# First projections of a two-block transformer kernel: from rstd-scaled, column-form products to raw rows scaled on eviction

## The chip, the cores and the metric

The kernel runs on one core of a Trainium2 chip. The time is the device time of one execution in microseconds, the median of several runs; lower is better.

## What is computed

Two transformer blocks on one sequence of 256 tokens of width 1024, in 32-bit floats. The part around the change is the start of the first block, cut here from the reference:

```python
def rmsnorm(x, g):
    xf = x.astype(jnp.float32)
    y = xf * lax.rsqrt(jnp.mean(xf * xf, axis=-1, keepdims=True) + EPS)
    return (y * g.astype(jnp.float32)).astype(x.dtype)

h = rmsnorm(x, pre_mix_g[l])
aq, ak, av, hq, hf_fwd, hf_bwd, hi, hg = split_columns(h @ w_in[l], IN_SPLITS)
...
f = lb_dir + (1.0 - lb_dir) * jax.nn.sigmoid(z.astype(jnp.float32))
qf = heads(jax.nn.silu(q.astype(jnp.float32)), HG_HEAD_K)
o = bidirectional_gated_scan(qf, log_forget(zf_fwd, lb[0]), log_forget(zf_bwd, lb[1]), heads(i_in, HG_HEAD_V))
```

Here z is hf_fwd or hf_bwd and q is hq; the scan runs over the tokens in both directions. Then come cross attention to a memory `mem` of 256 rows, a feed-forward block with a convolution, and a second block of the same width.

## The kernel before

The sequence is two row tiles (R = 2) of 128 tokens; the width is eight tiles (KT = 8) of 128. Every 32-bit product is made of three: operands are split into a high part (rounded, fp32r) and a low part (the rest), and high x high, low x high and high x low are accumulated in PSUM. Weights come by SyncE's DMA queue into a ring of two slots of 2 MB, and are split in **pieces** of 128 x 1024 elements (512 KB): ScalarE's `ahead` writes the high part (L1630), VectorE's `ahead` the low part (L2265). Pieces are numbered in the order hff, hfb, hq, aq, akv, hi, hg, xkv0, ...; each of these has four, akv two. A piece has one of three places, so its high part waits until the piece three before it is used.

TensorE takes the pieces in two forms. `cols_half` (column form, L578 and L742) keeps a 128 x 128 weight tile stationary and streams the turned activations, 256 columns; the result has features on the partitions. A piece is 24 such products. `gemm_rows` (row form, L578 and L635) keeps the turned activations stationary and streams 512 weight columns; tokens are on the partitions. A piece is 12 products. A `turn` (L753) is four 128 x 128 transposes into one PSUM bank. Banks 0 to 3 (G) are for projections in turn, 4 to 7 (M) for turns, scores and scan levels; `take` waits until a bank's last readers are done.

Start: SyncE loads x, then the weights of hff and hfb; ScalarE issues the load of the columns (identity, gains) and, later, of the tables. ScalarE squares x by rows (L1646), GpSimd makes rstd (L1500, L1501), VectorE scales (L2277), TensorE turns (L775), ScalarE evicts high parts (L1661) and VectorE low parts (L2287) of `hT1`, with the gain. A few matmuls on zeros run meanwhile (L765). GpSimd issues the loads of the positions (L1528) and row vectors (L1530). Behind its first low parts VectorE makes the rotary angles (L2323 to L2342), which wait for tables and positions, then further low parts (L2343).

Then hff and hfb in column form, the turns of mem, and hq in column form. ScalarE applies sigmoid and silu on eviction (L1694); VectorE's `forget` makes f from it (L2365), ScalarE the keys 1 - f (L1729), GpSimd products of f over blocks (L1541). The scan works in nine levels (L830, L816): each is 32 or 16 small matmuls, behind which VectorE doubles queries (L2421) and keys (L2411) and keeps the result (L2396, L2388), and ScalarE gathers keys (L1723). To hide this, TensorE gets projection pieces as filler behind each level (`after_level`). Behind level 8 come the turns of q and k of the attention, one filler, and the value products of the scan (L872, L874).

## Time and profile before

| | |
|---|---|
| median of 3 runs | 892.42 us (892.14 to 893.91) |
| span of the profiled execution | 891.2 us (its own time is not listed) |
| TensorE busy | 879.5 us, 99% |
| VectorE busy | 648.1 us, 73% |
| ScalarE busy | 494.0 us, 55% |
| GpSimd busy | 92.7 us, 10% |
| read from memory | 150.35 MB, 170 GB/s over the span |
| first product of hff | 11.89 us |
| level 0 of the scan | 53.09 us |
| first value product of the scan | 114.80 us |

In the rows below, the first two numbers of a timeline row are the start and the length in us; "x16" is the number of instructions merged; brackets give how long the engine was idle before and what ended it. PE is TensorE's matmuls, PEld its weight loads, DVE VectorE, ACT ScalarE, POOL GpSimd, SP SyncE; an engine's name with a q is its instruction queue, where DMAs are issued. Names such as sb_ta are tiles in SBUF (sb_ta holds `hT1`), ps are PSUM banks.

### The profile page before, as it was taken

The page shows a single profiled execution, that of the slowest core. Times are in us where ns is not written, and L with a number is a line of the kernel's source. Part 1 is how long each engine was busy: PE and PEld are TensorE (multiplying, and loading weights), DVE is VectorE, ACT ScalarE, POOL GpSimd, SP SyncE. Part 2 cuts the span into 40 slices and gives each one's busy share as a digit, 9 for nine tenths or more (in the row PEclk, how much of TensorE's full clock was granted, in tenths as well). Part 3 has the DMA queues.
Part 4 walks back from the last instruction along what each step waited for, and adds up shares of the span by engine and source line. Part 5 has one row for each costly group of instructions (what it writes and reads, how often), then busy time and mean ns, then how long its engine had stood idle before and what let it go on. Part 6 is the DMA issues. An engine that isn't in the chain of part 4 may idle for free.

```text
span 891.2 us, 13262 instructions
## 1 busy us (share of the span) xinstructions
PE 879.5 (99%) x5100; PEld 753.7 (85%) x5100; DVE 648.1 (73%) x1024; ACT 494.0 (55%) x880; POOL 92.7 (10%) x123
## 2 busy tenths in 40 slices
PE   8999999999999999999999999999999999999997
PEld 6988897889889888888789887898888888888885
DVE  5789975574879688789856846677787774766774
ACT  5954665464577465566635366676555772324341
POOL 1324100000010000000133300011030100000000
PEclk9999999999999999999999999999999999999999
DMA  9755424453664455556418644344366554564531
GB/s 317 245 168 176 155 95 139 146 201 106 189 212 143 142 181 186 201 188 238 166 60 286 210 142 142 107 166 166 96 232 193 175 180 142 189 212 166 189 142 48
DMA packets 99502, 152.25 MB, mean 171 GB/s; under 512 B 2608, under 2 KB 66352, under 8 KB 99184
## 3 DMA queue, kind: packets, MB, share of 16 engines
q1 hardware_dynamic: 99040, 150.68, 50.6%
q8 instruction: 41, 0.67, 0.3%
q10 hardware_dynamic: 288, 0.47, 0.2%
q0 software_dynamic: 112, 0.26, 0.1%
q14 instruction: 21, 0.17, 0.1%
HBM read 150.35 MB, written 1.05 MB: 170 GB/s over the span
## 4 chain that ended last, share of the span: by engine, by line
PE 90%; DVE 5%; ACT 2%; issue 1%; DMA 1%; POOL 0%; DVEq 0%; POOLq 0%; SPq 0%; ACTq 0%
PE ps L578 27%; PE ps L571 19%; PE ps L1079 13%; PE ps L635 7%; PE ps L1083 7%; PE ps L667 4%; PE ps L742 2%; PE ps L753 1%; DVE sb_wlo L2265 1%; PE ps L830 1%; ACT sb_whi L1630 1%; PE ps L706 1%; PE ps L1027 1%; PE ps L931 1%; PE ps L1223 1%
## 5 line engine op out<-in xcount | busy, mean ns | idle before, releaser
L2265 DVE TENSOR_TENSOR sb_wlo<-sb_ring,sb_whi 128x1024 fp32r<-128x1024 f32 (+2 forms) x169 | 203.6, 1216 | 81.2 <-ACT sb_whi L1630 80.8
L1630 ACT ACTIVATE sb_whi<-sb_ring 128x1024 fp32r<-128x1024 f32 (+2 forms) x169 | 174.0, 1045 | 101.3 <-PE ps L635 70.0
L578 PE MATMUL ps<-sb_whi,sb_tb 128*128 128x512 f32 (+2 forms) x520 | 137.7, 387 | 0.0
L578 PEld LDWEIGHTS ps<-sb_whi,sb_tb 128*128 128x128 f32 x520 | 94.1, 188 | 17.2 <-issue 1.0
L635 PE MATMUL ps<-sb_wlo,sb_tb 128*128 128x512 f32 (+2 forms) x224 | 66.6, 380 | 0.0
L578 PE MATMUL ps<-sb_whi,sb_ta 128*128 128x512 f32 (+1 forms) x240 | 61.4, 380 | 0.0
L1518 POOL TENSOR_SCALAR sb_st<-sb_st 128x1 f32<-128x1 f32 x14 | 7.3, 524 | 451.6 <-ACT sb_probs L1894 451.5
L2223 ACT ACTIVATE sb_b<-sb_b 128x512 f32<-128x512 f32 x9 | 5.7, 632 | 79.7 <-DVE sb_b L2694 79.7
L578 PEld LDWEIGHTS ps<-sb_whi,sb_ta 128*128 128x128 f32 x240 | 42.4, 188 | 8.6 <-issue 0.5
L635 PEld LDWEIGHTS ps<-sb_wlo,sb_tb 128*128 128x128 f32 x224 | 41.5, 188 | 7.8
L2694 DVE TENSOR_REDUCE sb_b<-ps 128x256 f32<-128x512 f32 x36 | 23.9, 686 | 28.6 <-PE ps L1083 28.6
L1997 ACT ACTIVATE sb_b<-ps 128x256 f32<-128x256 f32 x32 | 12.2, 381 | 52.7 <-PE ps L1083 52.7
L571 PE MATMUL ps<-sb_whi,sb_ta 128*128 128x512 f32 (+1 forms) x120 | 37.4, 377 | 0.1
L578 PE MATMUL ps<-sb_tb,sb_whi 128*128 128x256 f32 x256 | 35.1, 288 | 0.8 <-DVE sb_tb L2287 0.7
L578 PEld LDWEIGHTS ps<-sb_tb,sb_whi 128*128 128x128 f32 x256 | 32.0, 191 | 2.5 <-issue 1.6
L1709 ACT ACTIVATE sb_b<-ps 128x512 f32<-128x512 f32 (+1 forms) x44 | 24.2, 590 | 9.6 <-PE ps L742 4.6
L578 PE MATMUL ps<-sb_ta,sb_whi 128*128 128x256 f32 x192 | 26.6, 294 | 1.4 <-DVE sb_ta L2287 1.4
L2265 DVE TENSOR_TENSOR lent9lo<-sb_ring,lent9hi 128x1024 fp32r<-128x1024 f32 x19 | 23.2, 1220 | 5.9 <-ACT lent9hi L1630 5.9
L2265 DVE TENSOR_TENSOR lent1lo<-sb_ring,lent1hi 128x1024 fp32r<-128x1024 f32 x18 | 22.0, 1221 | 7.5 <-ACT lent1hi L1630 7.5
L635 PE MATMUL ps<-sb_wlo,sb_ta 128*128 128x512 f32 (+1 forms) x96 | 27.3, 372 | 0.0
L2754 DVE SCALAR_TENSOR_TENSOR sb_b<-sb_b,sb_col 128x255 f32<-128x255 f32 x64 | 26.6, 478 | 0.8 <-ACT sb_b L2015 0.8
L578 PEld LDWEIGHTS ps<-sb_ta,sb_whi 128*128 128x128 f32 x192 | 25.1, 201 | 1.7 <-issue 1.6
(430 smaller groups left out, 2065.0 us busy)
## 6 DMA issues: line engine op xcount, KB each, us to landing
sb_ring<-in_w_in SPq DMA_DIRECT2D x32, 1024.0 KB, 5.6
sb_ring<-in_w_up SPq DMA_DIRECT2D x18, 1024.0 KB, 5.1
sb_ring<-in_w_down SPq DMA_DIRECT2D x11, 1024.0 KB, 7.2
sb_ring<-in_w_ffn_down SPq DMA_DIRECT2D x11, 1024.0 KB, 7.5
sb_ring<-in_w_ffn_gate SPq DMA_DIRECT2D x9, 1024.0 KB, 5.3
sb_ring<-in_w_ffn_up SPq DMA_DIRECT2D x9, 1024.0 KB, 5.4
sb_ring<-in_w_xkv SPq DMA_DIRECT2D x8, 1024.0 KB, 5.6
sb_ring<-in_w_out SPq DMA_DIRECT2D x4, 1024.0 KB, 5.0
```

The costliest lines, as they stand in the source:

```text
L571: mm = pe.matmul(o, l[a_], r[b_], start=(start and n == 0), stop=(stop and n == 2), skip_group_check=not check)
L578: pe.matmul(o, l, r, start=(start and n == 0), stop=False, skip_group_check=True)
L635: mm = pe.matmul(o, T[0][:, k0 + i, r * P:(r + 1) * P], w[1][:, i], start=False, stop=k0 + i == k - 1, skip_group_check=True)
L667: mm = pe.matmul(o, T[0][:, k0 + i, r * P:(r + 1) * P], w[1][:, i], start=False, stop=k0 + i == k - 1, skip_group_check=True)
L742: mm = pe.matmul(o, w[1][:, i, :], T[0][:, i, :], start=False, stop=i == KT - 1, skip_group_check=True)
L1079: pe.matmul(o[:, :], w[0][:, k, :], both_halves[f][:, k].rearrange("p two n -> p (two n)"), start=k == 0, stop=False)
L1083: mm = pe.matmul(o[:, 0:S], w[1][:, k, :], T[0][:, k, :], start=False, stop=k == KT - 1)
L1630: act.activation(piece_pair(m)[0], src, ACT.Copy).then_inc(s("hi_done"), 1)
L1709: act.activation(dst, bank[banks.at[key][0]][:, 0:n], ACT.Copy, scale=1.0 if scale is None else scale).then_inc(banks.release(key), 1)
L2265: dve.tensor_tensor(low, pieces[m][1], high.bitcast(F32), ALU.subtract).then_inc(s("lo_done"), 1)
L2694: dve.tensor_reduce(dst[c], o[:, :].rearrange("p (two n) -> p n two", two=2), AX.X, ALU.add).then_inc(banks.release(key), 1)
L2754: dve.scalar_tensor_tensor(dst, src, COL[:, at:at + 1], dst, ALU.mult, ALU.add).then_inc(banks.release(key) if last and c and i < SPLIT_FR ...
```

## The change

The host passes a turned copy of x with the gains in front. ScalarE and VectorE split it, times the gain, straight into `hT1`, without rstd; the first chunk's loads are spread over ScalarE's and SyncE's queues. All projections of x are in row form on these unscaled tiles; rstd is the `scale` of the activation that evicts. The sigmoid of hff and hfb and the silu of hq are evicted as rows and turned by TensorE; `forget` reads the turned gates in PSUM, and turned hq is evicted by ScalarE. Plain x is still loaded, for its squares and the residual. The pieces behind the levels move one forward, and the columns, tables, positions and row vectors are loaded at other places.

```diff
+        turned_x = nc.alloc_sbuf_tensor_at("turned_x", [P, KT + KT * S], F32, offset=nc.sbuf_base - 4 * KT * 2 * S)
+        first_gain, xT = turned_x[:, 0:KT], turned_x[:, KT:].rearrange("p (k n) -> p k n", n=S)
+        hff_rows, hfb_rows, hq_rows = v3(B[1], 0, R, 512), v3(B[1], R * 512, R, 512), v3(B[2], NS, R, 512)
...
-        T_FORM = ("hff", "hfb", "hq", "xkv0", "xkv1", "w_xq0", "w_xq1")
+        FIRST = "hff"
+        T_FORM = ("xkv0", "xkv1", "w_xq0", "w_xq1")
+        def first_chunk(name, w):
+            slot_at[0] += 1
+            raw[name] = [v3(ring, q * PIECE, 2, 512) for q in range(4)]
+            chunks.append((name, [((q // 2,), [(raw[name][q], w[2 * q * P:2 * (q + 1) * P, :])]) for q in range(4)], KT, 512))
...
-            for cols in (512, 512, 512, 256):
+            for cols in (512, 512, 256):
...
-            for m in range(4):
-                banks.take(pe, f"pre_mix_g.{m}", M[m], 2)
-            for r in range(R):
-                for m in range(4):
-                    if m % 2 == 0:
...

+                piece_at[0] = 1
+                keys = [f"{FIRST}.{r}" for r in range(R)]
+                for key in keys:
+                    banks.take(pe, key, next_g())
+                def both_rows(k, T, w):
+                    for r, key in enumerate(keys):
+                        mm = pe.matmul(bank[banks.at[key][0]][:, :], T[:, k, r * P:(r + 1) * P], w[:, k, :],
+                                       start=k == 0 and T is hT1[0] and w is high, stop=False, skip_group_check=True)
+                    return mm
+                for k in range(2):
+                    pe.wait_ge(*(hi_done(0) if k else (s("first_w_hi"), 1)))
+                    pe.wait_ge(s("first_hi"), k + 1)
+                    both_rows(k, hT1[0], high)
+                    pe.wait_ge(s("first_lo"), k + 1)
+                    both_rows(k, hT1[1], high)
+                    pe.wait_ge(*(lo_done(0) if k else (s("first_w_lo"), 1)))
+                    mm = both_rows(k, hT1[0], low)
+                piece_used(0, mm)
+                for k in range(2, KT):
+                    waits_at[k, None] = [(s("first_lo"), k + 1)]
+            def turn_gate(name, src, at):
+                for r in range(R):
+                    pe.wait_ge(*banks.empty(f"{name}.{r}"))
+                for m in range(2):
+                    turn(f"{name}T.{m}", src, [2 * m, 2 * m + 1], M[at + m], 1)
+            first_piece()
+            gemm_rows("hff", hT1, (1, 4))
+            gemm_rows("hfb", hT1)
+            pe.wait_ge(s("col_in"), 16)
+            turn_gate("hff", hff_rows, 0)
+            gemm_rows("hq", hT1, (0, 2))
+            turn_gate("hfb", hfb_rows, 2)
+            gemm_rows("hq", hT1, (2, 4))
             turn_norm("mem_norm_g")
-            for half in range(2):
-                cols_half("hq", hT1, half)
+            gemm_rows("aq", hT1, (0, 1))
+            turn_gate("hq", hq_rows, 0)
+            gemm_rows("aq", hT1, (1, 2))
...
-            gemm_rows("aq", hT1, (0, 1))
-            after_level(0, (gemm_rows, "aq", hT1, (1, 3)))
-            after_level(1, (gemm_rows, "aq", hT1, (3, 4)), (gemm_rows, "akv", hT1, (0, 1)))
-            after_level(2, (gemm_rows, "akv", hT1, (1, 2)), (gemm_rows, "hi", hT1, (0, 1)))
-            after_level(3, (gemm_rows, "hi", hT1, (1, 3)))
-            after_level(4, (gemm_rows, "hi", hT1, (3, 4)), (gemm_rows, "hg", hT1, (0, 1)))
-            after_level(5, (gemm_rows, "hg", hT1, (1, 3)))
-            after_level(6, (gemm_rows, "hg", hT1, (3, 4)), (turned_tiles, "mem_norm_g"),
-                        (cols_half, "xkv0", memT, 0, (0,)))
-            after_level(7, (cols_half, "xkv0", memT, 0, (1,)), (cols_half, "xkv0", memT, 1, (0,)))
-            after_level(8, (turn_qk1,), (cols_half, "xkv0", memT, 1, (1,)))
+            after_level(0, (gemm_rows, "aq", hT1, (2, 4)))
+            after_level(1, (gemm_rows, "akv", hT1))
+            after_level(2, (gemm_rows, "hi", hT1, (0, 2)))
+            after_level(3, (gemm_rows, "hi", hT1, (2, 4)))
+            after_level(4, (gemm_rows, "hg", hT1, (0, 2)))
+            after_level(5, (gemm_rows, "hg", hT1, (2, 4)))
+            after_level(6, (turned_tiles, "mem_norm_g"), (cols_half, "xkv0", memT, 0))
+            after_level(7, (cols_half, "xkv0", memT, 1))
+            after_level(8, (turn_qk1,))
...
+            for q in range(4):
+                part = slice(KT * (q > 0) + 2 * q * S, KT + 2 * (q + 1) * S)
+                sp.dma_start(turned_x[:, part], a["turned_x"][:, part]).then_inc(s(f"turned_x_in{q}"), 16)
+            load_part(FIRST, 2)
+            load_part(FIRST, 3)
+            load_part("hfb", 0)
             for r in range(R):
                 sp.dma_start(x[:, r, :], a["x"][r * P:(r + 1) * P, :]).then_inc(s(f"x_in{r}"), 16)
-            load_all(names[:SLOTS])
+            load_part("hfb", 1)
+            load("hq")
             sp.dma_start(mem, a["mem"].rearrange("(r p) n -> p r n", p=P)).then_inc(s("mem_in"), 16)
             sp.dma_start(masks[:, :, :], a["masks"].rearrange("p (l n) -> p l n", n=BLOCK)).then_inc(s("masks_in"), 16)
-            load_all(names[SLOTS:])
+            load_all(names[SLOTS + 1:])
             o = out.rearrange("(r p) n -> p r n", p=P)
...
+            pool.wait_ge(s("first_hi"), KT)
             pool.dma_start(posi[:, :], a["positions_2"].rearrange("(r p) -> p r", p=P),
                           allow_slow_non_contiguous=True).then_inc(s("pos_in"), 16)
             pool.dma_start(SG[:, :], a["row_vectors"].partition_broadcast(P)).then_inc(s("sg_in"), 16)
+            for r in range(R):
+                sums, rstds = (t[:, r:r + 1] for t in stats["pre_mix_g"])
+                rstd("pre_mix_g", [(s("pre_mix_g_sq"), r + 1)], sums, D, rstds)
...
-            act.dma_start(ident_col[:, :], a["ident_col"]).then_inc(s("col_in"), 16)
+            for k in range(2):
+                act.dma_start(raw[FIRST][0][:, k, :], chunks[0][1][0][1][0][1][k * P:(k + 1) * P, :]
+                              ).then_inc(s(f"first_half_in{k}"), 16)
+            dst, w = chunks[0][1][1][1][0]
+            act.dma_start(dst, w.rearrange("(k p) n -> p k n", p=P)).then_inc(raw_sem[FIRST, 1], 16)
...
+                high = piece_pair(0)[0]
+                hi_at[0] = 1
+                for k in range(KT):
+                    if k < 2:
+                        act.wait_ge(s(f"first_half_in{k}"), 16)
+                        act.activation(high[:, k, :], raw[FIRST][0][:, k, :], ACT.Copy
+                                       ).then_inc(s("hi_done" if k else "first_w_hi"), 1)
+                    if k % 2 == 0:
+                        act.wait_ge(s(f"turned_x_in{k // 2}"), 16)
+                    act.activation(hT1[0][:, k, :], xT[:, k, :], ACT.Copy, scale=first_gain[:, k:k + 1]
+                                   ).then_inc(s("first_hi"), 1)
+                    if k in (3, 5, 7):
+                        ahead_of(FIRST, (k + 1) // 2)
+                    if k == 5:
+                        act.dma_start(ident_col[:, :], a["ident_col"]).then_inc(s("col_in"), 16)
+                        act.dma_start(cst[:, :], a["tables"]).then_inc(s("const_in"), 16)
+            first_tiles()
+            ahead_of("hff", 6)
+            for r in range(R):
+                act.wait_ge(s(f"x_in{r}"), 16)
...
             act.wait_ge(s("angles"), 2)
             act.activation(ropes[:, :, 0:32], ang[:, 0], ACT.Sin).then_inc(s("sincos"), 1)
             act.activation(ropec[:, :, 0:32], ang[:, 1], ACT.Sin).then_inc(s("sincos"), 1)
-            ahead_of("hff", 5)
+            ahead_of("hff", 7)
             act.wait_ge(s("lam_dots"), 1)
             act.activation(lam_e, lam_dot, ACT.Exp).then_inc(s("lam_exp"), 1)
             act.wait_ge(s("lb_shift"), 2)
             act.activation(lb_e, lb_e, ACT.Exp).then_inc(s("lb_exp"), 1)
+            ahead_of("hff", 8)
+            for r in range(R):
+                act.wait_ge(s("pre_mix_g_rstd"), r + 1)
+            def apply(name, r, dst, func):
+                key = f"{name}.{r}"
                 act.wait_ge(*banks.full(key))
-                act.activation(dst, bank[banks.at[key][0]][:, 0:512], func).then_inc(banks.release(key), 1)
+                act.activation(dst[:, r, :], bank[banks.at[key][0]][:, 0:512], func, scale=rstd1(r)
+                               ).then_inc(banks.release(key), 1)
+            for r in range(R):
+                apply("hff", r, hff_rows, ACT.Sigmoid)
+            ahead_of("hfb", 6)
+            for r in range(R):
+                apply("hfb", r, hfb_rows, ACT.Sigmoid)
+            ahead_of("hfb", 7)
+            def spread_keys(d, n):
                 for half in range(2):
-                    ahead_of("hfb", 5 + 2 * half)
-                    apply(f"hfb.{half}", FD[:, NS + half * 512:NS + (half + 1) * 512], ACT.Sigmoid)
-            pre_norm("mem_norm_g", mem, [[(s("mem_in"), 16)]] * R, memT, gain_at("mem_norm_g"), forget_hfb)
+                    act.wait_ge(*banks.empty(f"h{n}T.{half}"))
+                for half in range(2):
+                    lo = d * NS + half * 512
+                    act.activation(KD[:, lo:lo + 512], FD[:, lo:lo + 512], ACT.Identity,
+                                   bias=1.0, scale=-1.0).then_inc(s("k_ready"), 1)
+            spread_keys(0, "ff")
+            def before_mem():
+                ahead_of("hq", 4)
+                spread_keys(1, "fb")
+                ahead_of("hq", 5)
+                gather_keys(1)
+                for r in range(R):
+                    apply("hq", r, hq_rows, ACT.Silu)
...
+            pre_norm("mem_norm_g", mem, [[(s("mem_in"), 16)]] * R, memT, gain_at("mem_norm_g"), before_mem)
             ahead_of("hq", 6)
-            apply("hq.1", hq[:, 512:1024], ACT.Silu)
+            for m in range(2):
+                take_rows(f"hqT.{m}", hq[:, m * 512:(m + 1) * 512])
...
-                take_rows(f"aq.{r}", qkv[:, r, 0:512])
+                take_rows(f"aq.{r}", qkv[:, r, 0:512], scale=rstd1(r))
...
+            high, low = piece_pair(0)
+            lo_at[0] = 1
+            for k in range(KT):
+                if k < 2:
+                    dve.wait_ge(*(hi_done(0) if k else (s("first_w_hi"), 1)))
+                    dve.tensor_tensor(low[:, k, :], pieces[0][1][:, k, :], high[:, k, :].bitcast(F32),
+                                      ALU.subtract).then_inc(s("lo_done" if k else "first_w_lo"), 1)
+                dve.wait_ge(s("first_hi"), k + 1)
+                dve.scalar_tensor_tensor(hT1[1][:, k, :], xT[:, k, :], first_gain[:, k:k + 1],
+                                         hT1[0][:, k, :].bitcast(F32), ALU.mult, ALU.subtract).then_inc(s("first_lo"), 1)
+                if k in (3, 5, 7):
+                    ahead_of(FIRST, (k + 1) // 2)
             dve.wait_ge(s("col_in"), 16)
-            pre_norm("pre_mix_g", x, hT1, gain_at("pre_mix_g"), lambda: None, lambda: ahead_of("hff", 1))
-            ahead_of("hff", 4)
             dve.wait_ge(s("const_in"), 16)
             dve.tensor_copy(mask_rows[:, :], cst[:, C_QROW:C_QROW + 2 * P]).then_inc(s("mask_ready"), 1)
...
-            ahead_of("hfb", 1)
+            ahead_of("hfb", 2)
...
-                    dve.wait_ge(*banks.empty(f"h{name}.{half}"))
+                    key = f"h{name}T.{half}"
+                    o = psum(key)
-                        f = dve.tensor_scalar(t[:, j * S:(j + 1) * S], t[:, j * S:(j + 1) * S],
+                        f = dve.tensor_scalar(t[:, j * S:(j + 1) * S], o[:, j * S:(j + 1) * S],
                                               lb_left[:, c:c + 1], lb[:, c:c + 1], ALU.mult, ALU.add)
-                    f.then_inc(s(f"{name}_ready"), 1)
-            ahead_of("hfb", 3)
+                    f.then_inc(banks.release(key), 1)
+            ahead_of("hfb", 5)
             forget("ff", 0)
-            ahead_of("hfb", 5)
+            ahead_of("hfb", 7)
             def forget_hfb():
-                ahead_of("hq", 3)
                 forget("fb", 1)
+                ahead_of("hq", 5)
+                dve.wait_ge(s("k_ready"), 4)
+                dve.tensor_tensor(kdiag, KD[:, 0:NS], KD[:, NS:2 * NS], ALU.add).then_inc(s("kdiag"), 1)
             pre_norm("mem_norm_g", mem, memT, gain_at("mem_norm_g"), lambda: None, forget_hfb)
-            dve.wait_ge(s("k_ready"), 4)
-            dve.tensor_tensor(kdiag, KD[:, 0:NS], KD[:, NS:2 * NS], ALU.add).then_inc(s("kdiag"), 1)
-            ahead_of("hq", 5)
+            ahead_of("hq", 6)
```

## Rows read from the trace of the kernel before

**Rows 1.** The page: span, busy time of each engine, and the chain that ended last, by engine.
```profile
span 891.2 us, 13262 instructions
...
PE 879.5 (99%) x5100; PEld 753.7 (85%) x5100; DVE 648.1 (73%) x1024; ACT 494.0 (55%) x880; POOL 92.7 (10%) x123
...
PE 90%; DVE 5%; ACT 2%; issue 1%; DMA 1%; POOL 0%; DVEq 0%; POOLq 0%; SPq 0%; ACTq 0%
```

**Rows 2.** Stretches: start:end, length, busy of PE, PEld, DVE, ACT, POOL, clock, DMA share, GB/s.
```profile
2.70:10.00 7.30, 5.80 (x20) 2.89 (x20) 2.56 (x8) 3.54 (x6) 3.02 (x6) 1.00 1.08 339
6.70:11.90 5.20, 2.36 (x17) 1.74 (x17) 4.04 (x8) 3.98 (x9) 2.88 (x5) 1.00 1.14 327
12.30:15.60 3.30, 3.30 (x17) 3.18 (x16) 3.30 (x7) 2.44 (x4) 0.00 (x0) 0.50 1.09 341
16.40:53.00 36.60, 36.41 (x294) 35.53 (x292) 28.33 (x62) 28.89 (x44) 12.65 (x14) 1.00 0.64 210
50.00:70.00 20.00, 20.00 (x186) 17.09 (x185) 15.68 (x20) 10.00 (x13) 0.00 (x0) 1.00 0.70 237
70.00:100.00 30.00, 29.92 (x249) 24.61 (x249) 29.72 (x46) 15.80 (x23) 14.41 (x6) 1.00 0.45 141
```

**Rows 3.** TensorE's timeline: first piece, fifth piece, level 0, value products.
```profile
11.89 3.62 PE L578 MATMUL ps<-sb_ta,sb_whi 128*128 128x256 f32 x16 [1.35 <-DVE sb_ta L2287]
...
25.06 2.08 PE L578 MATMUL ps<-sb_ta,sb_whi 128*128 128x256 f32 x16
...
53.09 1.15 PE L830 MATMUL ps<-sb_b 128*64 128x64 f32 x32
...
114.80 0.27 PE L872 MATMUL ps<-sb_b 128*128 128x128 f32 x1
```

**Rows 4.** Groups of ScalarE's instructions from 0 to 60 us.
```profile
L1630 ACT ACTIVATE sb_whi<-sb_ring 128x1024 fp32r<-128x1024 f32 x17 | 17.8, 1068 | 8.4 <-PE ps L635 4.2 <-PE ps L742 3.5 <-DMA sb_ring<-in_w_in 0.6
L1694 ACT ACTIVATE sb_b<-ps 128x512 f32<-128x512 f32 x6 | 3.5, 594 | 1.2 <-PE ps L742 1.2
L1661 ACT ACTIVATE sb_ta<-ps,sb_col 128x256 fp32r<-128x256 f32 x8 | 3.0, 488 | 0.6 <-PE ps L775 0.6
...
L1694 ACT ACT_TABLE_LOAD x2 | 2.6, 1283 | 0.0
L1723 ACT ACTIVATE sb_b<-sb_b 128x512 f32<-128x512 f32 x4 | 2.5, 698 | 0.5 <-DVE sb_b L2411 0.5
```

**Rows 5.** TensorE's timeline: a column piece, turns of mem, halves of a row piece.
```profile
22.18 2.08 PE L578 MATMUL ps<-sb_ta,sb_whi 128*128 128x256 f32 x16
...
36.93 1.96 PE L753 MATMUL ps<-sb_col,sb_b 128*128 128x128 f32 x16 [0.19 <-DVE sb_b L2277]
38.65 2.16 PE L578 MATMUL ps<-sb_ta,sb_whi 128*128 128x256 f32 x16
...
57.02 1.07 PE L578 MATMUL ps<-sb_whi,sb_ta 128*128 128x512 f32 x4
...
58.38 1.07 PE L578 MATMUL ps<-sb_whi,sb_ta 128*128 128x512 f32 x4
```

**Rows 6.** Loads issued from 0 to 60 us: KB each, us from issue to landing.
```profile
sb_b<-in_mem SPq DMA_DIRECT2D x1, 1024.0 KB, 13.1
...
sb_cst<-in_tables ACTq DMA_DIRECT2D x1, 272.0 KB, 6.2
...
sb_posi<-in_positions POOLq DMA_DIRECT2D x1, 1.0 KB, 5.6
```

**Rows 7.** Timelines of GpSimd, VectorE and ScalarE: positions, angles, sine, a low part.
```profile
8.66 0.95 POOL L1528 DMA_DIRECT2D sb_posi<-in_positions  x1
...
18.92 0.29 DVE L2323 CAST sb_maskrows<-sb_cst 128x256 bf16<-128x256 f32 x1
...
22.03 0.26 ACT L1680 ACTIVATE sb_ropes<-sb_probs 128x64 f32<-128x64 f32 x1 [2.98 <-DVE sb_probs L2342]
...
52.32 1.22 DVE L2265 TENSOR_TENSOR sb_wlo<-sb_ring,sb_whi 128x1024 fp32r<-128x1024 f32 x1
```

100 lines of the change are left out of this document (37 added, 63 removed).

## Prediction

> **What bounds the kernel now.** I read the page first: TensorE is busy 99% of the span and its instructions are 90% of the chain that ended last [rows 1]. So time is won or lost where TensorE starts late, waits, or gets more or less work; other engines matter where they feed it. Next I read the granted clock and the data rate of the start [rows 2], then TensorE's timeline [rows 3]. The first product of the first projection starts at 11.89 us, its fifth weight piece at 25.06, level 0 of the scan at 53.09 and the scan's value products at 114.80. After that TensorE hardly waits, so a shift at 114.80 should reach the end. The clock stood at 1.2 GHz from 12.3 to 15.6, after a stretch in which TensorE was busy 2.36 of 5.20 us. Lastly, VectorE is busy 29.72 of 30 us between 70 and 100 [rows 2]: inside the scan it is nearly a second bound.
>
> The profiled execution, whose own time isn't listed, has a span of 891.2 us, 1.2 below the median of the runs, 892.42; I take that 1.2 as constant. From no change a measurement of this kernel can tell about 0.2%, 1.8 us.
>
> **Removed at the start.** The path x, squares, rstd, scaling, 16 transposes, eviction ended at 11.89. Now TensorE needs the first quarter of turned x and a 256 KB weight block. The start moves 339 GB/s from 2.7 us on [rows 2]. Together these are 0.53 MB, so they land at about 4.5; ScalarE's half piece (0.6, as an eviction of 512 columns) and tile (0.38) give first products at about 5.6 [rows 4]. Weight piece 1 is behind 2.1 MB in all, lands near 9.0, and its high part takes 1.07: 10.1. Pieces 2 and 3 land near 10.5 and 12.0, ahead of need.
>
> **Row form against column form.** A half piece in row form takes 1.36 us, from 57.02 to 58.38, so a piece takes 2.73; a column piece takes 2.88, from 22.18 to 25.06 [rows 5]. That is only 0.15 a piece, 1.65 for the eleven pieces of hff, hfb and hq behind the first. Against it stand 24 new transposes: 16 took 1.72 us (36.93 to 38.65) [rows 5], so 24 take 2.6, with six starts of groups 3.1. The form by itself loses 1.4; all gain must come from the start.
>
> **The new wait.** TensorE runs pieces 1 to 3 from 10.1 to 18.6 (3 x 2.73 and 0.3 for a low part) and the first four products of piece 4 (0.9) until 19.5. Then it wants piece 4's low part, which VectorE makes only after the rotary angles. These need the tables and the positions. Both loads are issued later than now. ScalarE issues the column and table loads behind turned tile 5 and piece 2: piece 1 until 10.1, tiles 10.8, piece 2 11.8, then two issues, taken at 0.4 each, GpSimd's being 0.95 [rows 7]: 12.6. The tables, issued at 12.2, take 6.2 us to land as now: 18.4 [rows 6]. GpSimd's positions load waits for all eight turned tiles (13.3) and takes 5.6 [rows 6]: 19.0. VectorE has finished piece 3 at 15.6 and stands still; behind it stand its angles, the low parts of 4 and 5, and ScalarE's sine. From the mask copy at 18.92 to the sine at 22.03 the angles took 3.1 us: 22.1, and with 1.22 for the low part [rows 7] TensorE goes on at 23.4. TensorE waits 3.9 us. In the kernel before, the positions were issued at 8.66 and landed some 5 us before VectorE came to them at 18.92: that cover is gone. Piece 4 thus behaves as if started at 22.5, against 25.06: of the 6.3 us of earlier start 2.6 are left.
>
> The least that the wait can be is 1.6, where both loads are there when VectorE is free (column vectors about 16, 0.65 for the bounds, 3.1 angles, 1.2 low part); at the most it is 3 us more than I take, should the loads queue as mem's did, which needed 13.1 us for 1 MB [rows 6]. I take the rows' own 5.6 and 6.2, as the queues are as full at 12 to 19 as they were at 6 to 15 (327 and 341 GB/s) [rows 2]. The Trainium skill, DMA: Bandwidth & Descriptors, section Anatomy of one DMA, gives a fixed cost of about 2.0 us and bytes over 436 GB/s; by it the positions land at 15.4 and my sum would be 2.3 us lower, no change. The rows of this start show nearly three times that for a load of 1 KB, and the measurement decides.
>
> **From piece 4 to level 0.** Before: 28.0 us (25.06 to 53.09) for eight column pieces, one row piece and the mem transposes. After: ten pieces (a second aq piece comes ahead of level 0) 27.3, gate turns 3.1, mem transposes 1.7, 0.2 for the start of the level, and waits. For the waits I laid ScalarE's queue out from hq's end H (about 46.8): it gathers keys (1.3), loads the Silu table (1.28) and evicts hq (2 x 0.55), since it is held before that by VectorE's forget of hfb; only then come eight mem tiles (8 x 0.38), the high part of aq's second piece (1.0) and the turned hq [rows 4]. That high part is ready near H + 6.9. TensorE has 1.7 + 2.73 + 1.0 = 5.5 of work until it wants it. So it waits about 1.4 there, split between the turns of hq (mem banks 0 and 1 must be emptied) and the piece; I add 0.3 for its low part and 0.5 for hq's last low part: 2.2, bounded by 0 (ScalarE an instruction earlier) and 4. Sum 34.5, level 0 at 57.0: 3.9 later than 53.09.
>
> **Moved and hidden.** The levels keep two pieces each, the last filler (2.88) behind level 8 goes away, because one piece more was done ahead of level 0: minus 2.9. Its cover isn't needed: turning q and k follows, and the level's eviction ends under it. In the levels VectorE comes to its query products about 1 us later against level 0 than now, as it sits behind the same turns, and has 20.0 minus 15.7 us of idle time in 50 to 70 [rows 2]: I take 1.3 of new waits, between 0 and 3. The x squares and rstd are hidden (x lands near 20, the rstd is there near 23, first use is at about 28 on ScalarE). ScalarE's queue gains three weight loads ahead of all else, the split of piece 0 (two halves of 0.6 for 1.07) and two evictions of turned hq (0.6 each); VectorE loses the four scalings of x, and its forget reads PSUM where it read SBUF, some 0.05 an instruction. Both had idle time in the stretch from 16.4 to 53 (28.89 and 28.33 of 36.6 busy) [rows 2], so only what lies on the way around H is charged. The second megabyte of x costs 3 us of transfer; that is paid in the landings above; later it is covered, as mem's load, issued within 10 us of the start, landed 13.1 later [rows 6] and was wanted near 36. Scaling on eviction replaces a constant. GpSimd's products of f start some 3 us later than now and aren't wanted until level 2. SP issues the four quarters of turned x ahead of everything, and plain x only behind half of hfb; nothing there is wanted sooner than it lands.
>
> **The clock.** In the row 2.36 busy us of 5.20 were followed by 3.3 us at 1.2 GHz, which cost half of them, 1.65 [rows 2]. The new standstill is 3.9 us: between 0 and 1.65, I take 0.4, as it is shorter. A fall at the start would be free: it is absorbed in the wait for piece 4. The Trainium skill, TensorE: Matmul & The Clock Gate, section PE-mode transpose, says that transposes don't count as busy; the stretch before the fall held only transposes, which agrees. By it the start stays at 2.4 GHz, which changes nothing in the sum.
>
> **Sum:** +3.9 + 1.3 - 2.9 + 0.4 = +2.7: 892.4 + 2.7 = 895.1 us.
>
> **Rivals.**
> Small loads early: tables and positions are there when VectorE wants them, 1.6 of wait in place of 3.9, and no fall of the clock. 892.4 - 2.3 - 0.4 + 2.7 = 892.4, no change. For it: the positions are 1 KB. Against: 5.6 us in the row. 0.2; with the forecast's spread this is nearly all of "same".
> TensorE is fed throughout (the other side): VectorE's angles don't hold piece 4 back, as lands and issues come some us earlier than I laid out, and the waits of 2.2 and 1.3 don't arise. Place: piece 4's low part; it decides from its end before about 20.5. 892.4 + 2.7 - 0.4 - 3.9 = 890.8, and with the other waits gone 887.3; I name 889.0. Chance 0.24. For it: VectorE works only 28.3 of 36.6 us from 16.4 to 53 [rows 2].
> The clock falls in full: the standstill is followed by 3.3 us at half rate, as before: 895.1 + 1.25 = 896.3, and with late small loads 898. Chance 0.2.
> The lead is swallowed in the scan: should level 0 come early, VectorE at 29.72 of 30 us holds the levels, and only the moved filler counts: 889.5. It lies within the second rival.
> That row form isn't in fact 0.15 cheaper, or turns cost 0.13 each as in small groups, moves the sum by under 1.
>
> **Numbers.** Forecast and its spread 0.36, small loads early 0.2, fed 0.24, clock 0.2. Faster by over 1.8 us: 0.24. Within 1.8: 0.23 (0.2, and a little of the forecast). Slower: 0.53. The range leaves out one in ten at each side: 888.8 to 897.6. Cases of both signs are near each other; the likeliest alone has 893.3 to 896.8.
>
> **What would show it.** First real product near 5.6, piece 1 near 10.1; a wait of TensorE for VectorE's low part of about 4 us ending near 23.4, and VectorE's idle time before the mask copy released by a DMA; row pieces of 2.73; six turns of 0.43 to 0.5; waits of 1 to 2 us around the turns of hq behind ScalarE; level 0 near 57.0; no piece between level 8 and the value products at 117. It is wrong if the tables and positions land before 16, if level 0 stands before 54, or if the levels take much more than 56 us.

## The result and the profile after

The changed kernel takes 897.10 us (median of 4 runs, 896.98 to 897.26) against 892.52 us of the kernel before on the same chip (4 runs, 892.14 to 893.91): ratio 1.0049, interval 1.0036 to 1.0061. It is slower, by 4.6 us; 2.7 were forecast. The spans of the two profiled executions differ by 4.1 us.

The page of the changed kernel, beside [rows 1]: span, busy time by engine, and the chain that ended last.

```profile
span 895.3 us, 13001 instructions
...
PE 880.7 (98%) x4962; PEld 745.3 (83%) x4962; DVE 647.2 (72%) x1021; ACT 496.4 (55%) x883; POOL 89.3 (10%) x123
...
PE 83%; DVE 8%; ACT 4%; DMA 2%; issue 2%; POOL 0%; ACTq 0%; DVEq 0%; POOLq 0%; SPq 0%
```

TensorE's share of the chain has fallen from 90% to 83%; VectorE's has grown from 5% to 8%, ScalarE's from 2% to 4% and DMA's from 1% to 2%, some 18 us. So I looked for waits that one of these three ends, and first for those that a DMA ends.

TensorE's timeline of the changed kernel, the lines that answer to [rows 3] and [rows 5] (pieces are numbered from 0, hff's four being 0 to 3):

```profile
6.33 1.36 PE L791 MATMUL ps<-sb_whi,sb_ta 128*128 128x512 f32 x4 [0.26 <-ACT sb_ta L1726]
...
10.38 1.18 PE L591 MATMUL ps<-sb_whi,sb_ta 128*128 128x512 f32 x4 [0.82 <-ACT sb_whi L1673]
...
13.58 1.07 PE L591 MATMUL ps<-sb_whi,sb_ta 128*128 128x512 f32 x4
...
18.27 1.20 PE L591 MATMUL ps<-sb_whi,sb_ta 128*128 128x512 f32 x4 [1.81 <-ACT sb_whi L1673]
...
23.01 1.16 PE L591 MATMUL ps<-sb_whi,sb_ta 128*128 128x512 f32 x4
...
46.78 0.74 PE L648 MATMUL ps<-sb_wlo,sb_ta 128*128 128x512 f32 x2 [1.21 <-DVE sb_wlo L2340]
...
55.42 1.19 PE L591 MATMUL ps<-sb_whi,sb_ta 128*128 128x512 f32 x4 [0.78 <-ACT sb_whi L1673]
...
58.74 1.15 PE L868 MATMUL ps<-sb_b 128*64 128x64 f32 x32
...
118.80 0.46 PE L908 MATMUL ps<-sb_b 128*128 128x128 f32 x2
```

The first real product starts at 6.33 in place of 11.89, and piece 2 at 13.58. Then the lead goes: piece 3 waits until 18.27 for ScalarE's high part, and piece 4 (hfb's first) starts only at 23.01. Level 0 starts at 58.74, 5.65 us later than before, and the value products at 118.80, 4.0 later. From there on nothing changes: 4.0 of the 4.1 us of the spans are there.

Piece 3 is late although its load is the sixth issue of SyncE's queue, behind the four quarters of turned x and part 2 of hff. SyncE's queue tells why; its timeline, and then the table of its waits:

```profile
2.57 11.85 SPq L1481 DMA_DIRECT2D sb_ring<-in_w_in  x3
14.47 0.98 SPq L1511 DMA_DIRECT2D sb_x<-in_x  x2
```

```profile
SPq L1481 <- DVE sb_wlo L2340: 13.2, 2, 10.3
```

Three issues cover 11.85 us, 10.3 of them a single wait for a low part that VectorE makes. It is `load_part("hff", 3)`. The bookkeeping of `raw_before` (L467 of the changed kernel) gives a load, as what it must wait for, the last load of the same half of the ring. Parts 2 and 3 of hff are both entered under half 1, though they fill different bytes of it, so part 3 waits until piece 2 has been split. Nothing needs that: it is a false wait. Behind it in the queue stand hfb's weights and x. The data rate has a hole for it:

```profile
GB/s 0 0 53 141 305 332 412 404 401 410 391 393 254 5 0 144 353 131 0 74 221 399 388 121 170 347 415 369 399 421 412 401 401 393 388 385 385 390 385 390
```

These are 40 slices of 0.75 us, so the rate is 5, 0 and 144 GB/s from 9.75 to 12, and again 0 and 74 from 13.5 to 15. Piece 3 lands at 17.2 and hfb's first half at 21.7.

The granted clock follows; stretches of the changed kernel, columns as in [rows 2]:

```profile
18.00:20.00 2.00, 1.66 (x5) 1.07 (x6) 1.71 (x6) 0.22 (x1) 0.00 (x0) 0.92 0.88 296
20.00:22.00 2.00, 2.00 (x6) 1.59 (x5) 1.76 (x11) 0.23 (x1) 0.00 (x0) 0.50 1.04 392
22.00:24.00 2.00, 2.00 (x7) 1.16 (x6) 1.86 (x7) 2.00 (x3) 0.00 (x0) 0.73 1.02 412
```

After the wait of 1.81 us piece 3 runs at 1.2 GHz for the most part and takes 4.74 us in place of 2.73. The last view is VectorE's timeline, beside [rows 7]:

```profile
18.25 1.23 DVE L2340 TENSOR_TENSOR sb_wlo<-sb_ring,sb_whi 128x1024 fp32r<-128x1024 f32 x1 [3.95 <-ACT sb_whi L1673]
...
19.75 0.28 DVE L2409 CAST sb_maskrows<-sb_cst 128x256 bf16<-128x256 f32 x1
...
22.86 2.36 DVE L2340 TENSOR_TENSOR sb_wlo<-sb_ring,sb_whi 128x1024 fp32r<-128x1024 f32 x2
```

VectorE stands still until 18.25, but it is ScalarE's high part of piece 3 that releases it and no small load. Then come the angles, and the low part of piece 4 is ready at 24.1. I had forecast 23.4, for another reason. So three things were candidates for the one stretch: the late landing, the angles with their loads ahead of the low part, and the clock. A second group of waits, at 46.78 and 55.42, stood around the turns of hq.

### The profile page after: what moved, and what is told of

Read it like the earlier page. It is cut to its first block, busy times and chain, and to the rows that moved or that the text cites. A ratio compares the mean times of both kernels' runs of the same rounds, so it can differ in the third digit from the quotient of the medians.

```text
span 895.3 us, 13001 instructions
## 1 busy us (share of the span) xinstructions
PE 880.7 (98%) x4962; PEld 745.3 (83%) x4962; DVE 647.2 (72%) x1021; ACT 496.4 (55%) x883; POOL 89.3 (10%) x123
## 4 chain that ended last, share of the span: by engine, by line
PE 83%; DVE 8%; ACT 4%; DMA 2%; issue 2%; POOL 0%; ACTq 0%; DVEq 0%; POOLq 0%; SPq 0%
PE ps L591 23%; PE ps L584 19%; PE ps L1115 13%; PE ps L1119 7%; PE ps L648 6%; PE ps L680 4%; DMA sb_ring<-in_w_in 2%; PE ps L755 2%; DVE sb_wlo L2340 2%; ACT sb_whi L1673 1%; PE ps L766 1%; PE ps L719 1%; PE ps L1063 1%; PE ps L967 1%; PE ps L1259 1%
## 5 line engine op out<-in xcount | busy, mean ns | idle before, releaser
L591 PE MATMUL ps<-sb_whi,sb_ta 128*128 128x512 f32 (+1 forms) x328 | 86.4, 388 | 3.4 <-ACT sb_whi L1673 3.4
L591 PEld LDWEIGHTS ps<-sb_whi,sb_ta 128*128 128x128 f32 x328 | 59.2, 190 | 16.9 <-ACT sb_whi L1673 4.9
L648 PE MATMUL ps<-sb_wlo,sb_ta 128*128 128x512 f32 (+1 forms) x140 | 42.5, 390 | 1.7 <-DVE sb_wlo L2340 1.5
L2072 ACT ACTIVATE sb_b<-ps 128x256 f32<-128x256 f32 x32 | 12.2, 381 | 52.7 <-PE ps L1119 52.7
L584 PE MATMUL ps<-sb_whi,sb_ta 128*128 128x512 f32 (+1 forms) x120 | 37.5, 377 | 0.1
L648 PEld LDWEIGHTS ps<-sb_wlo,sb_ta 128*128 128x128 f32 x140 | 25.3, 191 | 9.2 <-DVE sb_wlo L2340 4.6
L1792 ACT ACTIVATE sb_b<-ps 128x512 f32<-128x512 f32 x40 | 22.5, 606 | 7.5 <-PE ps L766 4.9
L584 PEld LDWEIGHTS ps<-sb_whi,sb_ta 128*128 128x128 f32 x120 | 21.9, 188 | 4.7 <-DVE sb_ta L2800 0.5
```

The source lines that it names most:

```text
L584: mm = pe.matmul(o, l[a_], r[b_], start=(start and n == 0), stop=(stop and n == 2), skip_group_check=not check)
L591: pe.matmul(o, l, r, start=(start and n == 0), stop=False, skip_group_check=True)
L648: mm = pe.matmul(o, T[0][:, k0 + i, r * P:(r + 1) * P], w[1][:, i], start=False, stop=k0 + i == k - 1, skip_group_check=True)
L1792: act.activation(dst, bank[banks.at[key][0]][:, 0:n], ACT.Copy, scale=1.0 if scale is None else scale).then_inc(banks.release(key), 1)
```

## The experiments

Level 0 and value products are read from TensorE's timeline of each run. The kernel before had medians of 892.46, 892.47, 892.70 and 892.81 us beside the four groups of runs.

### e1_no_false_wait, e2_small_loads_early, e3_both, e4_fix_low_first

e1 takes the false wait away:

```diff
                 if name == FIRST:
+                    raw_before[name, j] = []
```

e2 has only the small loads early: ScalarE issues columns and tables right behind its three weight loads, and GpSimd doesn't wait for the turned tiles.

```diff
-            pool.wait_ge(s("first_hi"), KT)
...
+            act.dma_start(ident_col[:, :], a["ident_col"]).then_inc(s("col_in"), 16)
+            act.dma_start(cst[:, :], a["tables"]).then_inc(s("const_in"), 16)
```

e3 has both. e4 has the edit of e1, and in place of earlier loads an altered order on VectorE:

```diff
+            ahead_of("hfb", 2)
             dve.wait_ge(s("const_in"), 16)
             dve.tensor_copy(mask_rows[:, :], cst[:, C_QROW:C_QROW + 2 * P]).then_inc(s("mask_ready"), 1)
```

> The changed kernel with one wait taken away: the fourth load of hff doesn't wait any more until VectorE has split the third (it goes to other bytes of the ring). In the changed kernel SyncE stood from about 3.5 to 13.54 us in that wait, and piece 3 of hff landed near 17. Theory A (two causes in series: behind the late load stand the late positions and tables): piece 3 lands near 12 to 13, TensorE no longer waits for it, but the positions still land near 19.8, VectorE's angles end near 22.9, and TensorE waits 4 to 4.5 us for the low part of piece 4 until about 24.1; piece 4 behaves as if started near 23.2 against 23.01 now, the clock falls behind that wait as it does now, and the time stays within 1 us of 897.1. Rival B (the late load is the only cause): the 1.8 us of standstill and the fall of the clock go, level 0 moves from 58.74 to about 55.2 and the time to about 893.6.

> The changed kernel with the small loads early: ScalarE issues columns and tables right behind its weight loads, GpSimd positions and row vectors at once. SyncE's false wait stays. Theory A: no gain by itself, since VectorE makes the angles behind the low part of piece 3, which still waits for its late load; the 0.7 MB more in the early queue may even push the weights back by up to 1 us. 896.6 to 898.1, level 0 between 58.3 and 59.8. Rival (the late positions are what held TensorE): piece 4 starts earlier and the time falls by 2 us or more, to 895 or below.

> Both together: no false wait and small loads early. Theory A: neither cause is left, so TensorE has no standstill over 1 us ahead of piece 5, the clock stays at 2.4 GHz, piece 4 starts near 19 instead of 23.01, and the 4 us come through to level 0 (about 54.7) and the end: 892.6 to 893.8. Rival C (ScalarE and VectorE, or the landings, are the next bound at once): piece 4 starts earlier but piece 5 to 8 wait for their parts, and less than half of it comes through: 895 or more.

> No false wait, small loads where the change put them, but VectorE makes the low parts of pieces 4 and 5 ahead of the angles. Theory A: TensorE doesn't hang on the positions any more; hfb's first half lands near 16.5, piece 4's low part is ready near 19, piece 4 starts near 19 to 19.5, the clock stays up, the time is as with both changes of the loads, 892.6 to 894. If the positions' place cost nothing (rival B), this is equal to the run that only takes the false wait away.

Measured: e1 896.49 us (5 runs), ratio to before 1.0040 (1.0027 to 1.0052). e2 897.69 (5 runs), 1.0054 (1.0042 to 1.0067). e3 894.48 (11 runs), 1.0020 (1.0011 to 1.0029). e4 892.19 (11 runs), 0.9992 (0.9983 to 1.0000).

The times of e1 and e2 lie in the range of their theory A. e3 is 0.7 us above its range and e4 0.4 us below.

In e1 the weights are there in time, and TensorE runs from 12.2 to 20.1 without a stop; then comes the wait that I had forecast. VectorE's and then TensorE's timeline of e1:

```profile
18.44 0.30 DVE L2410 CAST sb_maskrows<-sb_cst 128x256 bf16<-128x256 f32 x1 [1.49 <-DMA sb_cst<-in_tables]
```

```profile
22.88 0.73 PE L649 MATMUL ps<-sb_wlo,sb_ta 128*128 128x512 f32 x2 [2.81 <-DVE sb_wlo L2341]
```

The tables land at 18.4, to the tenth what the prediction said, but by luck: they were issued at 10.8 and not at 12.2, and took 7.6 us and not 6.2. Piece 4's low part is taken at 22.88. The 10.3 us of false wait were thus worth 0.6 us: what it held up was behind the angles anyway. The wait was also good for something. The loads of the changed kernel, and then of e1, KB each and us from issue to landing:

```profile
sb_cst<-in_tables ACTq DMA_DIRECT2D x1, 272.0 KB, 2.7
...
sb_col<-in_ident_col ACTq DMA_DIRECT2D x1, 187.0 KB, 2.5
```

```profile
sb_cst<-in_tables ACTq DMA_DIRECT2D x1, 272.0 KB, 7.6
...
sb_col<-in_ident_col ACTq DMA_DIRECT2D x1, 187.0 KB, 6.0
```

With SyncE's loads held back the small loads land in 2.5 and 2.7 us, with them running in 6.0 and 7.6. So each of the two faults hid the other: take one away and the other comes up. e2 shows it from the other side. Its small loads are early, the false wait keeps VectorE from piece 3 until 19.7, the angles come behind that, and it is even 0.6 us slower than the changed kernel, since columns and tables, issued right behind piece 1's weights, are now in flight beside them: these take 8.8 us to land in place of 7.6, and piece 1 starts at 11.56 in place of 10.38. e3 pays that 1.1 us too (piece 1 at 11.51), and comes to level 0 at 55.06 in its profiled execution, which took 893.52, 1.0 less than the median. e4 pays nothing. Its stretches, columns as in [rows 2]:

```profile
14.00:18.00 4.00, 4.00 (x19) 3.33 (x18) 3.03 (x7) 2.54 (x3) 0.96 (x2) 1.00 1.04 403
18.00:22.00 4.00, 4.00 (x20) 3.30 (x19) 3.65 (x16) 2.94 (x5) 1.68 (x4) 1.00 1.04 377
22.00:26.00 4.00, 4.00 (x19) 3.31 (x18) 2.50 (x8) 3.92 (x8) 0.00 (x0) 1.00 1.05 387
```

TensorE is busy throughout at 2.4 GHz, level 0 starts at 53.58 and the value products at 113.66. That is 5.1 us earlier than in the changed kernel, as the medians say (4.9). It is the prediction's second rival as far as piece 4 goes.

The same comparison prices the clock where the forecast wait stands alone. Stretches of e1 behind that wait, columns as in [rows 2]:

```profile
22.00:24.00 2.00, 1.12 (x4) 0.99 (x5) 2.00 (x3) 1.98 (x3) 0.00 (x0) 0.92 1.06 389
24.00:26.00 2.00, 2.00 (x6) 1.54 (x6) 1.93 (x6) 0.68 (x3) 0.00 (x0) 0.50 1.04 385
26.00:28.00 2.00, 2.00 (x8) 1.57 (x7) 1.08 (x3) 1.88 (x2) 0.00 (x0) 0.73 1.05 412
```

From piece 4's first low part to the turns of hff TensorE takes 11.72 us in e1 (22.88 to 34.60), with part of it at 1.2 GHz, and 9.97 in e4 (19.89 to 29.86), all at 2.4 GHz. The difference is 1.75 us, and 1.6 of it lie in the two half pieces that run at 1.2 GHz for the most part (2.35 and 1.98 us in place of 1.36). The fall behind the wait of 2.81 us thus cost some 1.7 us.

### f6_clock_kept, f7_low_first_alone

f6 is the changed kernel with products that keep TensorE busy while it waits for piece 3; f7 is the changed kernel with only VectorE's order of e4.

```diff
-            gemm_rows("hff", hT1, (1, 4))
+            gemm_rows("hff", hT1, (1, 3))
+            for _ in range(8):
+                pe.matmul(bank[G[3]][:, :], hT1[0][:, 0, 0:P], hT1[0][:, 0:2, :], start=True, stop=True)
+            gemm_rows("hff", hT1, (3, 4))
```

> The changed kernel with eight 128x512 products on data that is already there (into a bank that is free until hfb's second row half, their result overwritten) issued by TensorE between hff's third and fourth piece, where it idled 1.81 us before the clock fell to 0.50 for 2.7 us. Theory A (the late positions and tables stand behind everything else of the first 25 us): the clock stays at 1.0, hff's fourth piece takes 2.7 us in place of 4.7, hfb's first piece starts at 21.0 in place of 23.0, and then waits for its low part, which VectorE still has ready only at 24.1: level 0 at 58.4 to 58.7, time 896.8 to 897.1. Rival B (the granted clock is what costs): the two microseconds come back in full, level 0 at 56.7, time 895.1. Rival C (the added products are no cover, they only delay the fourth piece): above 897.3.

> The changed kernel with only VectorE's order altered: the low parts of hfb's first two pieces before its wait for the tables and the angles. The false wait on SyncE's queue stays. Theory A' (two waits in a row, each hidden by the other: the late fourth piece of hff, and behind it the late low part): hfb's low parts are ready early, but hff's fourth piece still starts at 18.3 and at half clock, and hfb's first piece at 23.0: gain 0 to 0.3 us, 896.8 to 897.1, though both edits together gave 4.9. Rival D (the order on VectorE is the whole gain of the run with both): 892.2 to 893.

Measured: f6 897.31 us (5 runs), ratio 1.0048 (1.0036 to 1.0061). f7 898.33 (5 runs), 1.0060 (1.0046 to 1.0073).

f6, a stretch and then two lines of TensorE's timeline:

```profile
20.00:22.00 2.00, 1.93 (x8) 1.24 (x8) 1.79 (x11) 0.05 (x1) 0.00 (x0) 1.00 1.04 414
```

```profile
18.56 1.19 PE L591 MATMUL ps<-sb_whi,sb_ta 128*128 128x512 f32 x4 [0.23 <-ACT sb_whi L1676]
...
23.06 1.21 PE L591 MATMUL ps<-sb_whi,sb_ta 128*128 128x512 f32 x4 [1.13 <-ACT sb_whi L1676]
```

The clock is at 1.00 where it was at 0.50, and piece 3 ends near 21.9. Then TensorE waits for piece 4 all the same, until 23.06 against 23.01. The two microseconds at 1.2 GHz cost the changed kernel nothing. What released that wait was not the low part I had expected but the high part: hfb's first half lands at 21.9 (21.7 in the changed kernel) behind the false wait. So a fourth cover lay over the same stretch. The time of 897.31 is 0.2 us above theory A's range and by its number rival C's, but the added products delayed nothing: piece 3 starts 0.3 us later because its load lands at 17.45 in place of 17.16.

f7 missed both expectations: it is 1.2 us slower. VectorE's and TensorE's timelines:

```profile
22.58 2.36 DVE L2340 TENSOR_TENSOR sb_wlo<-sb_ring,sb_whi 128x1024 fp32r<-128x1024 f32 x2 [2.45 <-ACT sb_whi L1673]
```

```profile
29.37 1.20 PE L591 MATMUL ps<-sb_whi,sb_ta 128*128 128x512 f32 x4 [0.67 <-ACT sb_whi L1673]
```

With the loads late, the low parts of pieces 4 and 5 stand in VectorE's queue until 22.58, and now the angles stand behind them: they end at 27.9 in place of 22.8. ScalarE's sine waits for the angles, and piece 6's high part, for which TensorE waits above until 29.37, stands behind the sine. The order that gives most of 4.9 us with the loads on time loses 1.2 us with them late.

### f5_aq_ahead, f8_forget_first, f9_silu_first, f10_third_low

These start from e4 and go for the waits around the turns of hq. ScalarE's timeline of e4 there:

```profile
40.56 1.15 ACT L1777 ACTIVATE sb_b<-sb_b 128x512 f32<-128x512 f32 x2 [3.72 <-DVE sb_b L2454]
...
43.80 1.28 ACT L1762 ACT_TABLE_LOAD   x1
45.10 1.27 ACT L1762 ACTIVATE sb_b<-ps,sb_st 128x512 f32<-128x512 f32 x2
46.25 3.03 ACT L1705 ACTIVATE sb_tb<-ps,sb_col 128x256 fp32r<-128x256 f32 x8
49.10 1.12 ACT L1674 ACTIVATE sb_whi<-sb_ring 128x1024 fp32r<-128x1024 f32 x1
```

ScalarE is idle for 3.72 us and then makes piece 13's high part (49.10) behind table, Silu and eight mem tiles, 0.78 us after TensorE wants it. f5 brings it forward on both engines (first ScalarE's `before_mem`, then VectorE's `forget_hfb`):

```diff
-                ahead_of("hq", 4)
+                ahead_of("hq", 6)
                 spread_keys(1, "fb")
-                ahead_of("hq", 5)
...
                 forget("fb", 1)
-                ahead_of("hq", 5)
+                ahead_of("hq", 6)
```

f8 has also a new order on VectorE:

```diff
+            def hq_and_forget():
+                ahead_of("hq", 4)
+                forget("fb", 1)
-            pre_norm("mem_norm_g", mem, memT, gain_at("mem_norm_g"), lambda: None, forget_hfb)
-            ahead_of("hq", 6)
+            pre_norm("mem_norm_g", mem, memT, gain_at("mem_norm_g"), hq_and_forget, lambda: ahead_of("hq", 6))
+            dve.wait_ge(s("k_ready"), 4)
+            dve.tensor_tensor(kdiag, KD[:, 0:NS], KD[:, NS:2 * NS], ALU.add).then_inc(s("kdiag"), 1)
```

f9 keeps f8's order but kdiag, which goes back ahead of the mem tiles. On ScalarE `gather_keys(1)` goes from ahead of the Silu to behind hq's copies, with `ahead_of("hq", 7)` ahead of it, and on VectorE `ahead_of("aq", 3)` takes the place of `ahead_of("aq", 2)` between the query products. f10 is f9 with f5's order on VectorE up to kdiag.

> The run with both repairs (892.19), and both of aq's first pieces split earlier: ScalarE's high parts of aq's first two pieces before the spreading of hfb's keys (it idled 3.7 us there), VectorE's low part of the second right behind the first. Theory E (the 0.78 us TensorE waits behind the turns of hq is ScalarE's queue of table load, Silu and eight mem tiles ahead of that high part): the wait goes, hq's last low part is unchanged (0.78 us stays), level 0 at 52.6 in place of 53.6, time 891.1 to 891.5. Rival F (VectorE, now 1.2 us later with kdiag and the mem tiles, takes its place: the turns of hq wait for the second mem tile): 892.0 to 892.6.

> As the run before, and VectorE's order around mem altered as well: the low part of hq's last piece first, then forget of hfb, then the scaling of mem (its rstd comes late), then aq's two low parts, the mem tiles, and kdiag last. Theory E: the wait of 0.78 us for hq's last low part goes too, the keys are spread 1 us or so earlier or no later, level 0 at 51.6 to 52.0, time 890.0 to 890.7. Rival G (level 0 then waits for kdiag or for hq's copies, or POOL's block products, which start 3 us later, hold a level up): 891.3 or more.

> From the run with VectorE's forget ahead of mem's scaling (891.81): kdiag is back ahead of the mem tiles; ScalarE takes the Silu of hq (and its table) right after the spreading of keys and gathers the keys for level 0 only behind the mem tiles and hq's copies; the split of the third piece of aq comes ahead of both, on VectorE between the two query products. Theory E: the turns of hq no longer wait for the second mem tile (0.66 us), the piece behind level 0 no longer waits for its low part (1.72 us, and its clock at 0.51 to 0.64 for 4 us): level 0 at 50.8 to 51.3, time 889.0 to 889.7. Rival G (gathering late holds level 1 up, or POOL's block products, 3 us later than in the best run so far, do): 890.6 or more.

> As the run before, but VectorE scales mem before hfb's forget, as in the best run so far (890.62), so POOL starts its block products 3 us sooner, and the 0.85 us wait for hq's last low part stays. Theory E: level 0 at 51.9 as in that run, the 0.50 us wait of the piece behind it gone: 890.0 to 890.4. Rival G (late gathering costs more than it gives): 890.8 or more. If this run beats its sister by more than 0.3 us, POOL's start is what decides.

Measured: f5 890.62 us (8 runs), ratio 0.9975 (0.9965 to 0.9985). f8 891.81 (11 runs), 0.9991 (0.9982 to 1.0000). f9 890.19 (6 runs), 0.9971 (0.9960 to 0.9983). f10 889.52 (5 runs), 0.9962 (0.9948 to 0.9976).

| | median | level 0 | value products | between |
|---|---|---|---|---|
| before | 892.52 | 53.09 | 114.80 | 61.71 |
| changed | 897.10 | 58.74 | 118.80 | 60.06 |
| e4 | 892.19 | 53.58 | 113.66 | 60.08 |
| f5 | 890.62 | 51.97 | 112.30 | 60.33 |
| f8 | 891.81 | 51.93 | 114.69 | 62.76 |
| f9 | 890.19 | 50.57 | 111.81 | 61.24 |
| f10 | 889.52 | 51.99 | 111.21 | 59.22 |

Level 0 and value products are those of the profiled execution. It is within 0.2 us of the median in all rows but two: f8's took 893.04, 1.2 us above its median, and that of before some 893.0, 0.5 above. In every run from changed to f10 the profiled execution ends 778.3 us behind the value products, so the differences all lie ahead of them.

f5 gained 1.57 us, more than expected: besides the 0.78 the low part behind it was no longer late, and the turns of hq started at once. f8 won the wait for hq's last low part and lost more elsewhere. TensorE's timeline and a stretch of f8:

```profile
47.92 1.35 PE L767 MATMUL ps<-sb_col,sb_b 128*128 128x128 f32 x8 [0.66 <-DVE sb_tb L2362]
...
55.92 1.15 PE L649 MATMUL ps<-sb_wlo,sb_ta 128*128 128x512 f32 x2 [1.72 <-DVE sb_wlo L2340]
```

```profile
56.00:58.00 2.00, 2.00 (x5) 1.61 (x6) 2.00 (x2) 0.00 (x0) 0.00 (x0) 0.51 0.00 0
```

kdiag behind the tiles made the query products and the low part behind them late; TensorE stood still for 1.72 us right behind level 0, and then ran at 1.2 GHz. This profiled execution loses 2.4 us in the levels against f5 (62.76 and 60.33); by the medians f8 loses 1.2, so half of it is of this execution alone. f9 mends both (0.32 us of the second is left), misses its range (889.0 to 889.7), and has the earliest level 0 of all, 1.4 us ahead of f10, and yet is 0.7 us slower. One line of its timeline shows a piece of that:

```profile
67.53 1.17 PE L592 MATMUL ps<-sb_whi,sb_ta 128*128 128x512 f32 x4 [0.93 <-ACT sb_b L1791]
```

TensorE comes to a bank that ScalarE has not emptied yet, being held by the chain keys, doubling, keys between it and VectorE. In f9 VectorE copies level 0 at 56.44, in f10 at 55.87, and the value products are apart by the same 0.6: in f9 that chain sets the pace from level 0 on, and arriving earlier on TensorE buys nothing. VectorE is later because its eight table products take 2.2 us in f9 and 1.2 in f10, and the first query product stands right behind them (50.73 and 50.15). f10's expectation had named GpSimd's start as what decides. Its products start at 41.54 in f9 and at 38.94 in f10 and end at 52.0 and 51.5, and no engine waits for them in either trace; whether they slow VectorE's table products is open, since they run beside them in both.

### f11_late_part_alone, f12_turns_twice

f11 has the edits of f10 around hq without the two repairs of the start. f12 is f10 with every transpose of hff, hfb and hq issued twice into the same bank:

```diff
-                for j, k in enumerate(tiles):
+                again = 2 if key[:4] in ("hffT", "hfbT", "hqT.") else 1
+                for j, k in list(enumerate(tiles)) * again:
```

> The changed kernel with neither of the two repairs of the first 25 us, and only the new order around the turns of hq of the fastest run (aq's first two pieces split ahead of the key spreading, Silu ahead of the gathering for level 0, aq's third low part between the query products). Theory H (the waits behind 44 us are a matter of their own: they do not depend on when TensorE arrives): the gain is that of the two versions with the repairs, 892.19 less 889.52, so 2.7 us: 894.3 to 894.7, with hfb's first piece still at 23.0 and its late fourth piece of hff. Rival I (they only show once TensorE is on time): gain under 1 us, above 896.1.

> The fastest run (889.52) with the transposes of hff, hfb and hq each issued twice into the same bank (24 more, 2.4 us at the 0.79 us that eight take). It prices the turns that the row form added. Theory J (a turn is on the path with its own time, but where TensorE waits 0.95 us for hq's last low part it takes nothing): level 0 later by 1.4 to 1.6, time 890.9 to 891.2. Rival K (on the path in full): 891.7 to 892.1. Rival L (VectorE's chain through the levels covers it: TensorE arriving 1.4 us earlier at level 0 gained nothing in the run before): under 890.3.

Measured: f11 894.68 us (11 runs), ratio 1.0021 (1.0012 to 1.0030). f12 891.06 (11 runs), 0.9978 (0.9969 to 0.9987).

The waits around hq are a matter of their own: without the repairs their removal gives 2.4 us (897.10 to 894.68), with them 2.7 (892.19 to 889.52). The two parts add up. f12 is 1.5 us slower than f10, level 0 is at 53.49, as expected. TensorE's timeline of f12 at the turns of hff:

```profile
30.01 1.91 PE L768 MATMUL ps<-sb_col,sb_b 128*128 128x128 f32 x16
31.68 1.17 PE L592 MATMUL ps<-sb_whi,sb_ta 128*128 128x512 f32 x4
```

and of f10:

```profile
29.90 1.03 PE L767 MATMUL ps<-sb_col,sb_b 128*128 128x128 f32 x8
30.69 1.17 PE L592 MATMUL ps<-sb_whi,sb_ta 128*128 128x512 f32 x4
```

Eight transposes take 0.79 us on TensorE (29.90 to 30.69), sixteen 1.67. Of the 2.6 that were added in f12, 1.5 reach the end; most of the rest went into the 0.95 us of f10's wait for hq's last low part, which is gone in f12. Rival L is out: in f10 it does cost when TensorE comes to level 0 later.

## Why the prediction was right and wrong

The sign and the range held, the range with 0.5 us to spare, and the forecast cause stood at the forecast place, but it was not the one that acted first. By the prediction's own steps:

**Removed at the start: half right.** First product 6.33 (5.6 forecast), piece 1 10.38 (10.1). "Pieces 2 and 3 land near 10.5 and 12.0, ahead of need" is the step that failed: piece 3 landed at 17.2. I had followed the bytes and the rate and not the waits of SyncE's queue, though the bookkeeping of `raw_before` stands unchanged around the lines that the diff adds. The prediction followed loads from queue to queue, but did not ask what an issue itself waits for.

**The new wait: right in place, 1.1 us too long, and shown only once the failed step was mended.** The low part of piece 4 came at 24.1 (23.4 forecast), but released by piece 3's. In e1 the forecast chain stands as written: tables at 18.4, angles, TensorE taken up at 22.88, but after 2.81 us of waiting in place of 3.9, as it stopped at 20.1 and not at 19.5. Its repair, VectorE's order, is worth the difference from e1 to e4, 4.3 us. The forecast's wait of 3.9 and clock term of 0.4 come to the same by luck: measured they are 2.81 and some 1.7. The Trainium skill's figure in DMA: Bandwidth & Descriptors, section Anatomy of one DMA, about 2.0 us and bytes over 436 GB/s, is given there for loads that GpSimd issues. For such a load, the positions, it gives 2.0 us, and the changed kernel shows 6.3 and e1 5.2. Carried over to ScalarE's columns and tables, which is an estimate beyond what the page states, it gives 2.4 and 2.6 us. The changed kernel shows 2.5 and 2.7 where the false wait held SyncE's loads back, and e1 6.0 and 7.6 where it did not: a figure of this size fitted only the loads that had the queues to themselves.

**Row form: right.** 1.36 us a half piece (13.58 to 14.94). **Turns: over-sized.** Three groups took 2.4 us in place of 3.1.

**From piece 4 to level 0: under-sized.** 35.7 us in place of 34.5. The waits were placed right and sized at 2.2. They are 1.4 for hq's last low part (45.4, where it was wanted, to 46.78), for which I had taken 0.5, 1.3 around the turns of hq (2.1 from their start at 53.29 to 55.42, less 0.79) and 0.6 in piece 13, together 3.3. f11 shows that 2.4 of them could be had back by order alone. Another 0.35 lie in piece 4's first half, whose low part was wanted near 23.9 and ready at 24.1, 0.2 in piece 6's first half (1.59 in place of 1.36), and 0.3 in the three pieces behind a turn, whose first half takes 1.45 to 1.47.

**Levels: right in sum.** Level 0 to value products went from 61.71 to 60.06, minus 1.65; the terms +1.3 and -2.9 made minus 1.6. TensorE's idle time there grew by 0.8 (0.33 to 1.14) and its busy time fell by 2.5 (61.38 to 58.92), so both terms were some 0.4 too large and their errors cancel.

**The clock: right that it would fall, wrong in the size.** The start stayed at 2.4 GHz. In the changed kernel the fall came a piece early, and f6 shows its price in that place as nothing. In e1, where the forecast wait stands alone, the fall costs some 1.7 us and not 0.4. I had taken less than 1.65 because the new standstill was shorter than the row's stretch; but in the row TensorE was idle for only 2.84 of the 5.20 us, and the forecast standstill was 3.9 us of nothing but idle time. The rival "clock falls in full" had the size of the fall right and came nearest to the median (896.3), the latter for the wrong reason.

**The base.** I took the profiled execution of before as 1.2 us under the median. The profiled runs shown here have a span 1.8 us under their own time (897.12 with 895.3), so the one with 891.2 took about 893.0, and 0.5 us of the difference between 4.6 and 4.1 is that.

The rival "fed throughout" was placed at 889.0; e4 reached it at the start (892.19, where the prediction had 890.8 for this part alone), and f10 with most of the waits around hq gone as well (889.52, 3.2 us faster than the 892.70 of before beside it, and 7.6 faster than the change as made). What it left out is that these waits do not go by themselves.

The whole answer to why 5.6 us of earlier start moved the end back by 4: the lead was spent on a false wait and on the angles, which lay over each other; then a group of waits around the turns of hq; 2.4 us of turns and one more piece ahead of level 0 (2.73) that is given back in the levels.

## What to carry to other kernels

Before pricing a load by bytes and rate, ask what its issue waits for: a queue's waits come from bookkeeping, and a load divided into finer parts can inherit a wait that its bytes don't need. Where several delays lie over one stretch, taking one away shows little (0.6 us here) and may show a loss (e2, f7), while two together give 4.9; so test them in pairs before calling one harmless. An order within an engine's queue is only good for one timing of its inputs: the same edit was worth 4.3 us with the loads on time and minus 1.2 with them late.

## What the runs showed of the hardware that I had not expected

The same two loads of 187 and 272 KB took 2.5 and 2.7 us while SyncE issued nothing, and 6.0 and 7.6 us where 391 GB/s were moving in all (10 to 14 us of e1). The load of positions, 1 KB on GpSimd's queue, took 6.3 us in the changed kernel and 5.2 in e1: it was issued at 13.51, when SyncE's loads went on again, so it had nothing of the gap. The granted clock fell to 0.50 behind a wait of 1.81 us in the changed kernel and to 0.51 behind one of 1.72 in f8; eight products issued into the first of these waits kept it at 1.00. That first fall had no price, as another wait lay over it; the fall to 0.50 in e1, behind a wait of 2.81 us, cost some 1.7.
